# A fused transformer pair: three Strassen groups of convolution inputs ahead of the second attention, and its filler spread over 13 chunks

## The reference, cut to what matters

```python
h = rms_norm(x, norm1_g)
proj = jnp.einsum('bsd,de->bse', h, w_in)
q, k, v, bg, cg, xc = jnp.split(proj, [1024, 2048, 3072, 4096, 5120], axis=-1)
y_attn = chunked_relpos_attention(q, k, v, q_norm_g, k_norm_g, rel_bias)
y_conv = gated_short_conv(bg, cg, xc, conv_w, conv_b)
...
q = rms_norm(q.reshape(b, nc, CHUNK, N_HEADS, HEAD_DIM), q_norm_g)   # per head
k = rms_norm(k.reshape(b, nc, CHUNK, N_HEADS, HEAD_DIM), k_norm_g)   # per head
scores = jnp.einsum('bnqhd,bnkhd->bnhqk', q, kb) * scale + bias
probs = jax.nn.softmax(jnp.where(valid, scores, NEG_INF), axis=-1)
out = jnp.einsum('bnhqk,bnkhd->bnqhd', probs, vb)
```

## Time and profile before

| what | value |
| --- | --- |
| runs | 2182.41, 2184.18, 2175.30 us (median 2182.41) |
| profiled execution | 2176.62 us, span 2174.9 us |
| TensorE busy | 2147.4 us, 10450 matmuls |
| VectorE busy | 1480.9 us |
| ScalarE busy | 950.3 us |
| GpSimd busy | 999.6 us |
| queries, keys and the group | about 531 to 681 us of the span for the steps discussed |
| second attention, first to last step | about 705 to 1262 us |

### The profile page before, as it was taken

How to read it: one execution, slowest core, us unless ns; L and a number is a source line. 1 busy time by engine, 2 the same in 40 slices (tenths; PEclk the granted TensorE clock), 3 DMA queues, 4 the chain that set the end, 5 groups by cost and what they waited for, 6 DMA issues and landing times.

```text
span 2174.9 us, 29102 instructions
## 1 busy us (share of the span) xinstructions
PE 2147.4 (99%) x10450; PEld 1788.1 (82%) x10450; DVE 1480.9 (68%) x2585; ACT 950.3 (44%) x1696; POOL 999.6 (46%) x701
## 2 busy tenths in 40 slices
PE   8999999999999999999999999999999999999999
PEld 8888888888777888888888888788878888788887
DVE  7776775255875666666666658642786777898886
ACT  5555425343232555555555531211555455533332
POOL 3232465454545331313132246547465655666564
PEclk9999999999999999999999999999999999999999
DMA  6320123332135332324243256315144445826433
GB/s 230 104 76 21 45 94 148 126 117 101 55 116 156 103 94 88 99 77 112 67 109 82 75 185 248 115 49 184 59 132 157 167 150 180 328 93 227 151 121 116
DMA packets 198606, 269.34 MB, mean 124 GB/s; under 512 B 58136, under 2 KB 116280, under 8 KB 198368
## 3 DMA queue, kind: packets, MB, share of 16 engines
q1 hardware_dynamic: 124880, 201.38, 27.1%
q10 hardware_dynamic: 73616, 66.49, 10.0%
HBM read 191.23 MB, written 85.00 MB: 127 GB/s over the span
## 4 chain that ended last, share of the span: by engine, by line
PE 82%; DVE 8%; ACT 3%; issue 3%; POOL 2%; DMA 1%; ACTq 1%; POOLq 0%; DVEq 0%; SPq 0%
PE ps L204 71%; PE ps L2333 3%; PE ps L2308 2%; PE ps L2320 2%; PE ps L776 1%; PE ps L751 1%; PE ps L762 1%; DVE k_lo L2553 1%; POOL w_lo L3191 1%; DVE a_lo L446 1%; POOL w_lo L1887 1%; DVE qkv_head_stat L2145 1%; PE ps L2345 1%; DVE pt_lo L2601 0%; ACT pt_hi L2487 0%
## 5 line engine op out<-in xcount | busy, mean ns | idle before, releaser
L204 PE MATMUL ps<-a_hi,w_hi 128*128 128x512 f32 x1376 | 537.1, 407 | 6.0 <-POOL w_lo L1887 3.7
L159 POOL TENSOR_TENSOR w_hi<-w_raw,zero 128x512 fp32r<-128x512 f32 x172 | 201.2, 1200 | 735.9 <-PE ps L204 612.4
L204 PE MATMUL ps<-a_hi,w_lo 128*128 128x512 f32 x1376 | 516.9, 393 | 0.0
L204 PE MATMUL ps<-a_lo,w_hi 128*128 128x512 f32 x1376 | 514.0, 391 | 0.0
L204 PE MATMUL ps<-w_hi,a_hi 128*128 128x512 f32 (+1 forms) x960 | 369.4, 385 | 7.3 <-POOL w_lo L1887 3.5
L204 PE MATMUL ps<-w_hi,a_lo 128*128 128x512 f32 (+1 forms) x960 | 367.6, 383 | 0.0
L204 PE MATMUL ps<-w_lo,a_hi 128*128 128x512 f32 (+1 forms) x960 | 367.5, 383 | 0.0
L204 PEld LDWEIGHTS ps<-a_hi,w_lo 128*128 128x128 f32 x1376 | 258.4, 188 | 57.6
L204 PEld LDWEIGHTS ps<-a_hi,w_hi 128*128 128x128 f32 x1376 | 258.9, 188 | 50.0 <-POOL w_lo L1887 4.5
L204 PEld LDWEIGHTS ps<-a_lo,w_hi 128*128 128x128 f32 x1376 | 259.8, 189 | 40.8
L164 POOL TENSOR_TENSOR w_lo<-w_raw,w_hi 128x512 fp32r<-128x512 f32 x172 | 243.9, 1449 | 3.4
(11 more groups left out here) (307 smaller groups left out, 3938.1 us busy)
## 6 DMA issues: line engine op xcount, KB each, us to landing
mlp_part<-u_parts SPq DMA_DIRECT2D x26, 1024.0 KB, 7.9
w_raw<-in_w_in_dram SPq DMA_DIRECT2D x24, 1024.0 KB, 5.3
feat_fm<-stage ACTq DMA_DIRECT2D x68, 256.0 KB, 2.1
u_parts<-mlp_acc SPq DMA_DIRECT2D x28, 512.0 KB, 2.8
u_parts<-res SPq DMA_DIRECT2D x28, 512.0 KB, 2.8
conv_in<-feat_fm ACTq DMA_DIRECT2D x24, 512.0 KB, 5.1
res<-in_x_dram SPq DMA_DIRECT2D x16, 512.0 KB, 6.5
w_raw<-in_w_out_dram SPq DMA_DIRECT2D x8, 1024.0 KB, 5.0
```

Of the source, the lines that this page charges most:

```text
L159: hi = nc.gpsimd.tensor_tensor(w_hi[slot][:, k:k + 2, :], w_raw[:, k:k + 2, :], zero[:, 0:1].unsqueeze(2).to_broadcast([P, 2, CW]), ALU.add)
L204: last = nc.tensor.matmul(out_of(o), lhs, rhs(o), start=first and n == 0, stop=final and n == 2)
```

## The change

There are three groups of convolution inputs behind the keys instead of one, 21 group products instead of 7. Groups alternate between two sets of raw weight tiles and two sets of result quarters, and only the last one ends with the first filler chunk and the operand's conversion. The filler shrinks from 17 to 13 chunks, its 48 products behind the first chunk are spread evenly over all 130 steps (8.86 matmuls a step), the copies and stores of products come where their last part is done, and all eight pairs are written out on every engine. The norms of the third and fourth finished quarter of a unit move back: those of steps 5 and 6 of the queries from steps 6 and 7 to 7 and 8, that of step 12 of the keys from step 13 to 14, and that of step 13 within step 14 from ahead of the sum for m5 to behind it. The bank pair of a group product is counted from the last group, so that the first product, step 14, uses the pair after the one that step 13 fills last, and waits for step 13's second add.

```diff
-        BCX_GROUPS = 1
+        BCX_GROUPS = 3
+        FILL_CHUNKS = 13
...
-                    g, i = (s - NS) // 7, (s - NS) % 7
+                    g, i = (s - NS) // 7, s % 7
                     return i if i < 4 else i - 4 if g < NG - 1 else (2, 3, 2)[i - 4]
...
+                def pair(s):
+                    return (s - G_LAST) % 4 if s < G_LAST + 4 else (0, 1, 0)[s - G_LAST - 4]
...
+                def chunk_sides(g):
+                    return (as_chunk(rc), as_chunk(rb)) if g % 2 else (w_raw[:, :, :], as_chunk(rd))
...
+                def home(g, r):
+                    return (1, 1 - r) if g % 2 else (0, r)
...
+                def acc_free(eng, g, r):
+                    eng.wait_ge(*(store_q[home(g, r)].at(16 * UNITS) if g < 2 else b_store[r].at(16 * (g - 1))))
...
+                def normed_in(s):
+                    n = s - 1 if s % 7 in (4, 5) else s - 2 if s >= 7 and s % 7 in (0, 1) else None
+                    return n
...
         # SyncE
+                        elif NG > 1:
+                            load_group(1, 0)
                         store_quarter(u, (0, 0))
...
+                        if g + 2 < NG:
+                            load_group(g + 2, 0)
+                            load_group(g + 2, 1)
+                        elif g + 2 == NG:
+                            load_first()
+                        else:
+                            load_weights(sp, W_BCX2 + 1, W_BCX2 + 2)
...
         # TensorE, group products
+                        if before is None:
+                            pe.wait_ge(*added.at(added_to(NS - 2 + pair(s) // 2, 1 + 2 * (pair(s) % 2))))
+                        else:
+                            if before % 7 in COPIED:
+                                pe.wait_ge(*b_copied.at(b_copied_to(before)))
+                            if before % 7 in ADDED:
+                                pe.wait_ge(*b_added.at(b_added_to(before)))
...
         # ScalarE, group products
+                        if s == NS:
+                            squares(NS - 2)
+                        if not ends:
+                            weight_high(s + 2)
+                        elif i in (0, 1, 3, 4):
                             weight_high(s + (2 if i < 2 else 1))
+                        if s == NS + 1:
                             squares(NS - 1)
...
+                        if s == NS + 2:
                             root(NS - 1)
+                        if ends and i == 4:
...
+                            weight_high(s + 2)
                         if i in COPIED:
                             copy_group(s)
+                        if s == NS:
+                            root(NS - 2)
...
         # VectorE, group products
+                        i, ends = s % 7, s >= G_LAST
                         if i == 0:
                             weight_sum(position(s, "m6"))
-                            norm_heads(NS - 1)
+                            if s == NS:
+                                norm_heads(NS - 2)
                             weight_sum(position(s, "m5"))
+                            if s == NS:
+                                norm_heads(NS - 1)
                         elif i == 3:
                             weight_sum(position(s, "m4"))
-                        elif i == 5:
+                        elif i == 6 and not ends:
+                            weight_sum(position(s + 1, "m7"))
+                        if i in ADDED:
+                            add_group(s)
+                        if ends and i == 5:
                             dve.wait_ge(*plain_hi.at(1))
+                            dve.wait_ge(*low_w.at(NP))
...
         # phase_attention
+            FILLED = 4 * (fill_chunks - 1)
+            PARTS = 2 * (STEPS * pairs + 2)
+            def filled_to(part):
+                return FILLED * KB * part // PARTS
...
-                feed(block, w_start, 2 * pairs + 1, lambda j: (mm_h, j * 4 + 4))
+                feed(block, w_start, fill_chunks, lambda j: (mm_h, j * 4 + 4))
...
-                    with eng.Fori(0, pairs - 2) as j:
-                        body(j + 1, False, False)
-                    body(pairs - 1, False, True)
+                    for i in range(pairs):
+                        body(i, i == 0, i == pairs - 1)
...
+                            step = STEPS * i + n
+                            if step in STORE_AT:
+                                product_store(STORE_AT[step])
+                            if step in OUT_AT:
+                                product_out(OUT_AT[step])
                             high()
```

More of the change, by code:

```diff
@@ L1767, in place, with user_before @@
                 def place(s):
[L1769 removed]
+                    g, i = (s - NS) // 7, s % 7
                     return i if i < 4 else i - 4 if g < NG - 1 else (2, 3, 2)[i - 4]
[L1772 to L1774 removed]
+                def pair(s):
+                    return (s - G_LAST) % 4 if s < G_LAST + 4 else (0, 1, 0)[s - G_LAST - 4]
+                def user_before(s, where):
+                    return max((n for n in range(NS, s) if where(n) == where(s)), default=None)
                 def weight(side, s):
@@ L1961, in weight_high @@
                         elif s >= NS:
-                            before = place_before(s)
+                            before = user_before(s, place)
                             if before is None:
@@ L2032, in _ @@
                             copy_tile(s, 0)
-                        if squared_now:
-                            root(s - 1)
+                        if ready is not None:
+                            root(ready)
                         if i in COPIED:
@@ L2176, in _ @@
                             weight_sum(position(s + 1, "m7"))
-                        if s and (s - 1) % 7 in DONE:
-                            norm_heads(s - 1)
+                        if normed_in(s) is not None:
+                            norm_heads(normed_in(s))
                         if i == 2 and s >= 7:
@@ L2368, in product, with product_part @@
                             last.then_inc(mm_h, 1)
-                    def product_part(i, n, h, last):
-                        part = 2 * n + h
-                        ends = (8 * KB * part // TAIL, 8 * KB * (part + 1) // TAIL) if last else (2 * part, 2 * part + 2)
-                        for x in range(ends[0] // KB, (ends[1] - 1) // KB + 1):
-                            ks = range(max(ends[0] - x * KB, 0), min(ends[1] - x * KB, KB))
-                            product(i * 2 + (w_start + 1 + x // 4), x, ks, i * 8 + (EARLY + x))
+                    def product_part(i, n, h):
+                        part = 2 * (STEPS * i + n) + h
+                        begin, end = filled_to(part), filled_to(part + 1)
+                        for x in range(begin // KB, (end + KB - 1) // KB):
+                            ks = range(max(begin - x * KB, 0), min(end - x * KB, KB))
+                            product(w_start + 1 + x // 4, x, ks, EARLY + x)
                     for x in range(EARLY):
@@ L2628, in body @@
                             link.close(PER)
-                    pair_loop(dve, body)
-            products = 8 * pairs + EARLY
-            return ([(st_h[s], 16 * (4 * pairs + EARLY // 2 + 1)) for s in range(2)],
+                    pair_loop(body)
+            products = FILLED + EARLY
+            return ([(st_h[s], 16 * (products // 2 + 1)) for s in range(2)],
                     [[(o_done, 8 * pairs + 1), (ev_h, products - 1)], [(ev_h, products), (lo_r, 4 * pairs + 1)],
```

159 lines of the change are left out of this document (70 added, 89 removed).

## The result

The changed kernel takes 2212.09 us (median of 4 runs, 2211.04 to 2213.22), the kernel before 2180.64 (4 runs, 2175.30 to 2184.18): a ratio of 1.0146, 95% interval 1.0125 to 1.0167. It is 31.5 us slower. The profiled executions differ by more, 2212.45 against 2176.62 us. The forecast was slower, 2200 us in 2183 to 2222: the side and the range are right, the size is not. I had the loss at 19.4 us. The kernel before was timed anew with each batch of experiments, with medians of 2177.67 to 2180.64 us, so differences between kernels of different batches are good to about 3 us.

The account below looks back on a forecast made before the run. TensorE was taken to set the pace in the projection stage, a ring of VectorE and ScalarE in the attention. Terms +76.9 - 46 - 12.5 + 1 = +19.4 us on 2179.6, rounded up to 2200 us, range 2183 to 2222.

Parts of the forecast that it names:

- Matmuls moved (+76.9): Projection stage: two more groups add 336 matmuls at 0.229 us each, on the path, so +76.9 us.
- pauses (-12.5): Projection stage: moving the norms back removes TensorE's four pauses and the slow clock after them, -12.5 us, bounds 0 and 12.5.
- What the attention gives back (-46): Second attention: taking out 384 filler matmuls, 88.9 us of TensorE's time, saves 46 us, between 35 and 63.
- a ring of VectorE and ScalarE: Attention: the two engines pass work to and fro once a step, with no link waiting for TensorE.
- the rival that TensorE alone bounds it: Attention: all 88.9 us of removed filler come back, total 2155 us; chance 0.08.
- The upper bound, 63: Attention: at most 63 us saved, with TensorE never late and 16 copies fewer, leaving 494 us.
- the low end of 35: Attention: only 35 us saved, if the last pair's gain was mostly its two moved copies.
- TensorE's lateness falls from about 2.1 us to some 0.5: Attention: per eight steps, the time TensorE holds up others falls by 1.6 us, part of the -46.
- 2.47 us less of TensorE's work brought 1.26 us, 51%: Attention's last pair, with less filler, over eight steps; at this rate the 88.9 us removed give 45.
- The clock kept its level in the attention: Rival: longer TensorE pauses lower its clock in the attention, costing 11 to 27 us, about 2219 us; chance 0.10.
- The norms did free the pauses: Rival: in the projection stage the moved norms don't free the pauses, no -12.5, about 2212 us; chance 0.10.
- The ring did not get shorter than I thought: Rival: written-out code and fewer copies shorten the ring, the attention gives the full 63 us, 2182 us; chance 0.14.

Follow-up runs that it names:

- experiment 2: Changed kernel with one group and 17 chunks, the operand's reload also moved up to wait only for the reduction of step 13's squares: 2160.00 us.
- experiment 3: Changed kernel with two groups and 15 filler chunks instead of three groups and 13: 2182.77 us.
- experiment 1: One group and 17 chunks with the projection stage's new order: 2171.91 us with the old attention, 2165.75 us with the changed kernel's attention.
- experiment 4: Changed kernel without the two low-part passes of the attention's filler products, 832 matmuls fewer, results coarser: 2221.46 us in one profile.
- experiment 5: ScalarE's filler copy moved behind the high part in the changed kernel: 2201.02 us; doubled there: 2232.47 us; doubled in the kernel before: 2198.51 us.
- experiment 6: Changed kernel with the same 48 filler products spread unevenly over a head's 16 half steps, less in steps 1 and 2: 2204.68 us.
- experiment 7: Changed kernel with a semaphore of its own for the load of each head's values: 2206.08 us.

## Why the prediction was right, and where its size was off

**Matmuls moved (+76.9) and pauses (-12.5).** Right: with +1 for small things +65.4, measured +63.4. Each holds by itself as well, 75.7 us for the two groups and 12.4 for the pauses (experiments 2 and 3). All four pauses are gone, and the two windows above show TensorE at 20.00 of 20.00 us at full clock. The reserve I gave for covered waits was not needed. The moved norms delayed what I had said: in the trace of the changed kernel VectorE waited 2.61 us for the root, and the sum for m5 came at 642.73, 12 us behind that for m6 at 630.57. With three groups it was covered. I did not foresee that this cover hangs on the number of groups: with one, the reload of the operand is uncovered, and the moved norms alone gave 7 us (experiments 1 and 2). That the full 12.5 came in the changed kernel owes something to luck.

**What the attention gives back (-46).** The mechanism was right, a ring of VectorE and ScalarE that filler doesn't shorten: experiments 3, 4 and 5 each contradict the rival that TensorE alone bounds it. The term was mis-sized: 27.7 us came back where I had 46, with what lies behind the last reduction. The upper bound, 63, held, the low end of 35 did not. By the rows that the bound came from it nearly adds up: the 18.8 us less that TensorE holds up the others, and 16 copies fewer at 0.49 us, 7.8 us, are 26.6. Three steps of its working failed.

- "TensorE's lateness falls from about 2.1 us to some 0.5": it fell by about 1.0 us of the 1.6. Steps 1 and 2 of a head together took 7.9 us before and take 6.9, where 5.9 to 6.1 are possible (experiment 6): they are still 3.3 to 4.0 and 3.32 us, as the even spread puts as much filler there as elsewhere. Laying it elsewhere gave 7.4 us.
- "2.47 us less of TensorE's work brought 1.26 us, 51%": the rate doesn't carry. Of the 1.26 us, step 4 gave 0.49 (3.06 us where it was 3.55) because it has no copy there. Step 2 gave 0.70 (3.31 where it was 4.01) and has no copy there either, but by experiment 5 a copy costs nothing in it, so I put this part down to TensorE being less late. The changed kernel's step 2 takes 3.32 us too: the filler taken out beyond the last pair's gave nothing more there. Measured, 27.7 of 88.9 us are 31%.
- The late load of one head, 6.0 us (experiment 7), was in no term. I had counted the loads of the projection stage and taken those of the attention as they were, though the change alters the steps at which a chunk's load is issued.

The first and the third are 13.4 of the 18.3 us missing, by the gains of experiments 6 and 7. The other 5 I can't place by a run of its own. The late copy's 11 us aren't part of the account, since the copies stood in the ring before, too.

**The rivals.** The clock kept its level in the attention but for one spell: 1.00 over the stretch, though TensorE's pauses add up to 47 us. Not this one, then; but the thin filler, with 0.85 over the stretch, showed that it is near. The norms did free the pauses. The ring did not get shorter than I thought in these runs: the attention gave 27.7 us and not 63. And the direction, given 0.78, came out.

## What to carry to other kernels

A share of 99% on one engine doesn't say that it alone sets the time: look for a ring of two other engines with no wait for the first in it, step by step, because here spare time in one step did not pay for work in another. Work that fills an engine's gaps is nearly free where it stands and costs its full length in a stage where that engine sets the pace, so saving 11 us of matmuls cost 77 in one place to gain 28 in another. And before taking filler out, try the opposite: lay it out by the length of each step (7 us here), and move what shares the ring with it behind the hand-over (11 us here, with a part of one late load in them).

## What the runs showed of the hardware that I had not expected

With 832 matmuls fewer, some 800 of them in a stretch of 528 us, that stretch got 10 us longer: TensorE stood still up to 3.8 us at a time, its mean granted clock in the stretch fell to 0.85, and the steps that were slow were those at the lower clock (experiment 4). The Trainium skill (TensorE: Matmul & The Clock Gate, "HAM oscillation — how this bites in real kernels") warns of such pauses in a kernel that waits for its loads; here they come from waits for VectorE. With pauses of at most 1.7 us for VectorE, as in the changed kernel, the clock stayed at the 2.4 GHz level, which bears on the Trainium skill's account of frequent small pauses (same page, "A second HAM failure mode: psum-queue depth-cycling"): 57 waits, 47 us in all, did not bring it down here. But the length of one pause doesn't tell it. In the changed kernel with the doubled copy a pause of 1.81 us for VectorE at 789.40 us was followed by the 1.2 GHz level, and in the kernel of two groups with late copies a longer one, 2.91 us at 897.98, was not:

```profile
791.00:793.00 2.00, 2.00 (x6) 1.61 (x6) 1.96 (x6) 0.57 (x1) 0.00 (x0) 0.50 0.00 0
```

```profile
898.00:903.00 5.00, 5.00 (x31) 4.43 (x32) 2.79 (x11) 2.18 (x6) 0.00 (x0) 1.00 0.40 111
```
